# Input and first weights in four pieces, multiplied in step, and a third chunk on the unnormed input

## What is computed

```python
h = rmsnorm(x, mix_pre_norm[l])
u = h @ w_in[l]
u_z, u_xbc, u_dt, u_ly, u_lx, u_g = jnp.split(u, list(IN_SPLITS), axis=-1)
y_a = ssd_mixer(u_z, u_xbc, u_dt, ...)      # causal conv of u_xbc, silu, then a state-space scan
...
g = jax.nn.sigmoid(u_g.reshape(b, s, N_BRANCHES, D_MODEL) + gate_b[l])
```

## Time and profile before

| what | before |
|---|---|
| median of three runs | 841.94 us (841.87 to 842.13) |
| the profiled execution: its time | 842.37 us |
| the profiled execution: its span | 840.5 us |
| PE busy, PEld busy | 828.2 us (99%), 742.4 us (88%) |
| DVE busy, ACT busy, POOL busy | 638.5 us (76%), 503.2 us (60%), 68.3 us (8%) |
| granted TensorE clock, mean | 0.999 |
| HBM over the span | 175 GB/s |

### The profile page before, as it was taken

How to read it: one execution, slowest core, us unless ns; L and a number is a source line. 1 busy time by engine, 2 the same in 40 slices (tenths; PEclk the granted TensorE clock), 3 DMA queues, 4 the chain that set the end, 5 groups by cost and what they waited for, 6 DMA issues and landing times. The chain is left out here.

```text
span 840.5 us, 14554 instructions
## 1 busy us (share of the span) xinstructions
PE 828.2 (99%) x5758; PEld 742.4 (88%) x5758; DVE 638.5 (76%) x1148; ACT 503.2 (60%) x828; POOL 68.3 (8%) x68
## 2 busy tenths in 40 slices
PE   8999999999999999999999999999999999999996
PEld 6999999999989988888888789899899888788885
DVE  6887987998968778878788859777655566776765
ACT  6575778665377755656556868853544363555443
POOL 0200002101020111111111200020000020001000
PEclk9999999999999999999999999999999999999999
DMA  8658443467465746555655455574333433465541
GB/s 299 235 180 285 156 150 109 151 213 285 143 206 161 242 162 210 180 197 176 203 182 197 153 174 199 151 252 151 126 110 118 152 101 101 148 203 181 195 151 51
DMA packets 42812, 147.81 MB, mean 176 GB/s; under 512 B 6876, under 2 KB 7672, under 8 KB 42232
## 3 DMA queue, kind: packets, MB, share of 16 engines
q1 hardware_dynamic: 42600, 146.75, 52.4%
q10 hardware_dynamic: 144, 0.13, 0.0%
HBM read 145.79 MB, written 1.08 MB: 175 GB/s over the span
## 5 line engine op out<-in xcount | busy, mean ns | idle before, releaser
L2000 DVE TENSOR_TENSOR t_wl<-t_raw,t_wh 128x1024 fp32r<-128x1024 f32 x256 | 312.6, 1230 | 84.1 <-ACT t_wh L1423 83.0
L1423 ACT ACTIVATE t_wh<-t_raw 128x1024 fp32r<-128x1024 f32 x256 | 268.1, 1055 | 93.9 <-PE bank L673 91.8
L673 PE MATMUL bank<-t_hx,t_wh 128*128 128x256 f32 (+1 forms) x1968 | 298.5, 302 | 0.3 <-ACT t_hx L1434 0.3
L673 PEld LDWEIGHTS bank<-t_hx,t_wh 128*128 128x128 f32 x1968 | 263.6, 191 | 13.3 <-issue 1.1
L673 PE MATMUL bank<-t_hx,t_wl 128*128 128x256 f32 x1136 | 160.1, 283 | 0.0
L673 PEld LDWEIGHTS bank<-t_hx,t_wl 128*128 128x128 f32 x1136 | 149.2, 192 | 3.0
L673 PE MATMUL bank<-t_wh,t_hx 128*128 128x512 f32 x440 | 122.4, 399 | 0.0
L673 PE MATMUL bank<-t_wh,t_br 128*128 128x512 f32 x384 | 103.9, 392 | 0.0
L673 PEld LDWEIGHTS bank<-t_wh,t_hx 128*128 128x128 f32 x440 | 80.9, 188 | 17.0 <-issue 0.9
L673 PEld LDWEIGHTS bank<-t_wh,t_br 128*128 128x128 f32 x384 | 70.9, 188 | 14.1 <-issue 0.2
L673 PE MATMUL bank<-t_wl,t_hx 128*128 128x512 f32 x220 | 68.3, 392 | 1.0 <-DVE t_wl L2000 1.0
(11 more groups left out here) (149 smaller groups left out, 680.1 us busy)
## 6 DMA issues: line engine op xcount, KB each, us to landing
t_raw<-in_ws SPq DMA_DIRECT2D x258, 512.0 KB, 4.0
t_br<-decay SPq DMA_DIRECT2D x1, 2048.0 KB, 8.8
t_arena<-in_post SPq DMA_DIRECT2D x3, 512.0 KB, 5.2
t_x<-in_xin SPq DMA_DIRECT2D x2, 512.0 KB, 5.1
t_bd<-in_bd SPq DMA_DIRECT2D x1, 1024.0 KB, 7.2
t_x<-in_xtok SPq DMA_DIRECT2D x1, 1024.0 KB, 6.6
t_arena<-in_mem SPq DMA_DIRECT2D x1, 1024.0 KB, 8.7
out<-t_x SPq DMA_DIRECT2D x3, 256.0 KB, 2.3
```

What stands on the lines that cost most here:

```text
L673: return e.matmul(o, l, r, start=st, stop=sp, skip_group_check=True)
L1423: e.activation(high(q), RAW[q % NR][:, :], ACT.Copy, bias=0.0, scale=1.0).then_inc(*hi.now(q))
L2000: e.tensor_tensor(low(q), RAW[q % NR][:, :], high(q).bitcast(F), SUB).then_inc(*lo.now(q))
```

## The change

The input x is loaded in four pieces of two k each (256 KB, rows of 2 KB), and units 0 and 1 in four pieces of 512 columns, alternating with them on SyncE's queue; the columns of `xbc4` are laid out so that piece i holds the weights of k = 2i and 2i+1 for all 256 output columns. ScalarE and VectorE do a piece of x and then its piece of weights, and TensorE multiplies dt and `xbc4` for these two k, four times. The four squares come behind all of this, with no split between them. `xbc0` moves ahead of `g0`, onto the unnormed input: it is now units 4 and 5, `g0` is 6 and 7, `g1` 8 and 9 as before. Its row factor is applied on VectorE as for `xbc4` and `xbc5`; its bank is 4 and its buffer `RAWX[2]`. `mix_sums` moves into `xbc5`, at (0, 3), and `norm_spread` in `xbc5` from (0, 6) to (1, 4). On ScalarE and VectorE, `xbc_first(4)`/`xbc_taps(4)` and `xbc_first(5)`/`xbc_taps(5)` now stand ahead of `g0`'s place in the walk. On VectorE the split of unit 4 moves from inside `h_parts` to ahead of it, and that of unit 5 from behind it to inside.

```diff
@@ stream_list
-    for i in (4, 5):
-        s.append((f"xbc{i}", "w_in", rng(XC_ + 256 * i, 256)))
+    for i in (4, 5, 0):
+        s.append((f"xbc{i}", "by_k" if i == 4 else "w_in", rng(XC_ + 256 * i, 256)))
...
@@ sp_program
-            for i in range(2):
-                e.dma_start(X[:, 4 * i:4 * i + 4, :], xin[:, 4 * i:4 * i + 4, :]).then_inc(s_x[i], 16)
-            fetch(0)
+            for i in range(4):
+                e.dma_start(X[:, 2 * i:2 * i + 2, :], xin[:, 2 * i:2 * i + 2, :]).then_inc(s_x[i], 16)
+                e.dma_start(RAW[i // 2][:, halves(i % 2)], ws[0, :, 512 * i:512 * i + 512]).then_inc(s_early[i], 16)
+            fetch(2)
             e.dma_start(conT[:, 0:NFIRST], con[:, 0:NFIRST]).then_inc(s_con, 16)
-            fetch(1)
+            fetch(3)
...
@@ pe_program
-            for k in range(8):
-                e.wait_ge(*d_xw.of(k))
-                mm(PB[6][0:32, 0:T], DTS[:, k, :], YBh[:, k, :], k == 0, False)
-                m = mm(PB[6][0:16, 0:T], DTS[:, k, 0:16], YBl[:, k, :], False, k == 7)
-            m.then_inc(*p_dt.now("dt"))
-            chunk("xbc4", YBh, YBl, {(0, 4): lambda: e.wait_ge(*hi.of(0)), (1, 6): mix_sums})
-            chunk("xbc5", YBh, YBl, {(0, 6): lambda: norm_spread("mix", 7)})
             for i in range(4):
-                if i == 0:
-                    chunk_by_units("g0", Hh, Hl, normed_high("mix"), normed_low("mix"))
-                    e.wait_ge(*d_const.of("row"))
-                else:
-                    chunk(f"g{i}", Hh, Hl)
+                if i % 2 == 0:
+                    q = walk.unit()
+                wh, wl = weights(q, 4)
+                for k in (2 * i, 2 * i + 1):
+                    e.wait_ge(*d_xw.of(k))
+                    mm(PB[6][0:32, 0:T], DTS[:, k, :], YBh[:, k, :], k == 0, False)
+                    m = mm(PB[6][0:16, 0:T], DTS[:, k, 0:16], YBl[:, k, :], False, k == 7)
...
+                e.wait_ge(*(hi.of(q) if i % 2 else hi.of(q, "first")))
...
+            chunk("xbc5", YBh, YBl, {(0, 3): mix_sums, (1, 4): lambda: norm_spread("mix", 7)})
+            chunk("xbc0", YBh, YBl)
+            chunk_by_units("g0", Hh, Hl, normed_high("mix"), normed_low("mix"))
+            e.wait_ge(*d_const.of("row"))
+            for i in range(1, 4):
+                chunk(f"g{i}", Hh, Hl)
                 chunk(f"xbc{i}", Hh, Hl)
...
@@ act_program
-            for k in range(8):
-                if k % 4 == 0:
-                    e.wait_ge(s_x[k // 4], 16)
-                act(YBh[:, k, :], X[:, k, :], ACT.Copy, scale=WMIX[:, k:k + 1]).then_inc(*a_xw.now(k))
-            split_by_halves(0)
+            for i in range(4):
+                e.wait_ge(s_x[i], 16)
+                for k in (2 * i, 2 * i + 1):
+                    act(YBh[:, k, :], X[:, k, :], ACT.Copy, scale=WMIX[:, k:k + 1]).then_inc(*a_xw.now(k))
+                split_early(i)
             for i in range(4):
                 act(SC0[:, 2 * i:2 * i + 2, :], X[:, 2 * i:2 * i + 2, :], ACT.Square).then_inc(*a_sq.now("mix", i))
-                if i == 1:
-                    split(1)
...
-            for i in range(4):
+            xbc_first(4)
+            walk.cols("xbc0")
+            xbc_first(5)
+            gates(0)
+            for i in range(1, 4):
                 gates(i)
-                xbc_first((4, 0, 1, 2)[i])
+                xbc_first(i - 1)
                 walk.cols(f"xbc{i}")
-                if i == 0:
-                    xbc_first(5)
...
@@ dve_program
-            walk.unit(1)
+            walk.unit(2)
             walk.tick()
-            h_parts("mix", SC1, X, WMIX, 7, {4: 4})
+            h_parts("mix", SC1, X, WMIX, 7, {4: 5})
...
-            for i in range(4):
-                walk.cols(f"g{i}", i == 0)
-                xbc_taps((4, 0, 1, 2)[i])
+            xbc_taps(4)
+            walk.cols("xbc0")
+            xbc_taps(5)
+            walk.cols("g0", True)
+            for i in range(1, 4):
+                walk.cols(f"g{i}")
+                xbc_taps(i - 1)
                 walk.cols(f"xbc{i}")
-                if i == 0:
-                    xbc_taps(5)
```

More of the change, by code:

```diff
@@ L201 @@
 NR, NS = 5, 4
+RAW_CHUNKS = {"xbc4": 0, "xbc5": 1, "xbc0": 2}
 MIDDLE = [name for name, _, _ in STREAM[[s[0] for s in STREAM].index("dnq0"):[s[0] for s in STREAM].index("gt3_0_0")]]
@@ L566, in evacuated @@
                 return (d_ev if name[0] == "vz" else a_ev if name[0][:2] in ("gt", "mv", "vu", "vv") else d_acc).of("free", *name)
-            if name[:2] in ("fu", "lx") or name[:3] in ("xbc", "dnq") and name not in ("xbc4", "xbc5"):
+            if name[:2] in ("fu", "lx") or name[:3] in ("xbc", "dnq") and name not in RAW_CHUNKS:
                 return d_cv.of(name)
@@ L636, in sp_program @@
                     e.wait_ge(s_decay[0], 16)
-                    e.wait_ge(*unit.of(LAST["xbc5"]))
+                    e.wait_ge(*unit.of(LAST["xbc0"]))
                     e.dma_start(ACS, decay.partition_broadcast(P)).then_inc(s_decay[1], 16)
@@ L681, in high_ready @@
             def high_ready(q):
-                e.wait_ge(*(hi.of(q) if q else hi.of(0, "first")))
+                e.wait_ge(*hi.of(q))
             def low_ready(q):
@@ L907, in ssd_lane @@
                     e.wait_ge(*a_silu.of(5))
-                    if g:
-                        e.wait_ge(*d_ssd.of("cb", 0))
+                    e.wait_ge(*(d_ssd.of("cb", 0) if g else d_ev.of("xbc0")))
                     mm(PB[4][:, 0:T], B[:, 0:128], C)
@@ L1231, in pe_program @@
             e.wait_ge(*d_dt.of("w"))
-            for k in range(8):
-                e.wait_ge(*d_xw.of(k))
-                mm(PB[6][0:32, 0:T], DTS[:, k, :], YBh[:, k, :], k == 0, False)
-                m = mm(PB[6][0:16, 0:T], DTS[:, k, 0:16], YBl[:, k, :], False, k == 7)
-            m.then_inc(*p_dt.now("dt"))
-            chunk("xbc4", YBh, YBl, {(0, 4): lambda: e.wait_ge(*hi.of(0)), (1, 6): mix_sums})
-            chunk("xbc5", YBh, YBl, {(0, 6): lambda: norm_spread("mix", 7)})
-            for i in range(4):
-                if i == 0:
-                    chunk_by_units("g0", Hh, Hl, normed_high("mix"), normed_low("mix"))
-                    e.wait_ge(*d_const.of("row"))
-                else:
-                    chunk(f"g{i}", Hh, Hl)
+            for i in range(4):
+                if i % 2 == 0:
[5 more added lines that the diff above has]
+                    m = mm(PB[6][0:16, 0:T], DTS[:, k, 0:16], YBl[:, k, :], False, k == 7)
+                if i == 3:
+                    m.then_inc(*p_dt.now("dt"))
+                cs = [(half(BANK["xbc4"], c), slice(128 * c, 128 * c + 128)) for c in range(2)]
+                e.wait_ge(*(hi.of(q) if i % 2 else hi.of(q, "first")))
+                for k in (2 * i, 2 * i + 1):
+                    for o, w in cs:
+                        mm(o, wh[:, k % 4, w], YBh[:, k, :], k == 0 and w.start == 0, False)
+                        mm(o, wh[:, k % 4, w], YBl[:, k, :], False, False)
+                e.wait_ge(*(lo.of(q) if i % 2 else lo.of(q, "first")))
+                for k in (2 * i, 2 * i + 1):
+                    for o, w in cs:
+                        m = mm(o, wl[:, k % 4, w], YBh[:, k, :], False, k == 7)
+                if i % 2:
+                    m.then_inc(*unit.now(q))
+                    walk.tick()
+            chunk("xbc5", YBh, YBl, {(0, 3): mix_sums, (1, 4): lambda: norm_spread("mix", 7)})
[4 more added lines that the diff above has]
+                chunk(f"g{i}", Hh, Hl)
                 chunk(f"xbc{i}", Hh, Hl)
@@ L1423, in split, with split_early @@
                 e.activation(high(q), RAW[q % NR][:, :], ACT.Copy, bias=0.0, scale=1.0).then_inc(*hi.now(q))
-            def split_by_halves(q):
-                e.wait_ge(s_raw[q], 16)
-                for c in range(2):
-                    e.activation(WH[q][:, halves(c)], RAW[q][:, halves(c)], ACT.Copy, bias=0.0,
-                                 scale=1.0).then_inc(*(hi.now(q) if c else hi.now(q, "first")))
+            def split_early(i):
+                q, c = i // 2, i % 2
+                e.wait_ge(s_early[i], 16)
+                e.activation(WH[q][:, halves(c)], RAW[q][:, halves(c)], ACT.Copy, bias=0.0,
+                             scale=1.0).then_inc(*(hi.now(q) if c else hi.now(q, "first")))
             walk = Walk(split)
@@ L2000, in split, with split_early @@
                 e.tensor_tensor(low(q), RAW[q % NR][:, :], high(q).bitcast(F), SUB).then_inc(*lo.now(q))
[L2002 to L2006 removed]
+            def split_early(i):
+                q, c = i // 2, i % 2
+                e.wait_ge(*(hi.of(q) if c else hi.of(q, "first")))
+                e.tensor_tensor(WL[q][:, halves(c)], RAW[q][:, halves(c)], WH[q][:, halves(c)].bitcast(F),
+                                SUB).then_inc(*(lo.now(q) if c else lo.now(q, "first")))
             walk = Walk(split)
@@ L2976, in lay_out @@
             v = i[c[0]][0][512 * c[1]:512 * c[1] + 512][:, c[2]].reshape(4, P, 512)
+        elif kind == "by_k":
```

(1 more changed line is left out.)

38 lines of the change are left out of this document (17 added, 21 removed).

## The result

| | before | after |
|---|---|---|
| median | 842.04 us (841.87 to 842.38, 4 runs) | 846.54 us (845.74 to 846.70, 4 runs) |
| profiled execution: time, span | 842.37, 840.5 us | 845.74, 843.9 us |
| granted TensorE clock, mean | 0.999 | 0.995 |

The ratio is 1.0051, with a 95% interval of 1.0039 to 1.0063: slower, as forecast, and inside the range. The sum was 3.25 us. Of profiled execution against profiled execution it is 3.37, of the medians 4.5.

What follows compares the result with a forecast made beforehand. TensorE was taken to bound the kernel from 26 us on. A 3.5 us head start less 6.6 to 6.7 us of waits made g1 3.25 us later: 845.2 us against the median, range 843.0 to 847.2.

Steps and rivals of the forecast that it cites:

- The sum: Whole kernel: g1 ends 3.25 us later, added to the profiled 842.37 gives 845.6, or 845.2 against the median.
- The mark at the end of g1: End of unit 9, behind which both orders are the same: 42.40 before, forecast 45.65 with the change.
- T: Start of the normed input on VectorE, forecast at 19.8 against 19.57 before.
- The start: ScalarE and VectorE up to the sums of squares: squares from 11.07, sums read at 15.99, 0.45 earlier than before.
- The landing: Loads of x and weights in pieces: last two at 9.7 and 10.4, nothing added for rows of 2 KB.
- the 1.5 us bound: Loads: the most that rows of 2 KB could delay the last piece, if each 512 KB lose 0.6 us.
- a rival of chance 0.10: Late pieces: rows of 2 KB cost 1.5 us at the last piece, normed input at 21.3, time 846.7; chance 0.10.
- the head start is spent on unit 4's split: VectorE ahead of the normed input: unit 4's split, 1.14 us, moved there, so the norm gains nothing.
- The waits: TensorE in g0 and g1: unit 7 waits 1.7 and 1.75 us, unit 9 waits 2.1 and 0.75.
- The rival of the clock: TensorE's new waits: clock falls to 1.2 GHz for half a unit, 1.4 us more, 846.6; chance 0.06.
- The gain comes through: g0 and g1: splits of units 7 and 9 on time, TensorE keeps its 3.5 us, 838.4; chance 0.10.

Runs made afterwards that it cites:

- the one with TensorE kept busy: The changed kernel with matmuls that nobody reads in TensorE's waits at units 7 and 9: 846.26 us, ratio 1.005 to the kernel before.
- the second profile: The changed kernel timed and profiled once more with no edit: 846.10 us, ratio 1.005 to the kernel before.
- the pieces alone: Loads and engine start of the change, with xbc0, its bank and the splits' order as in the kernel before: 843.66 us, ratio 1.0014.
- the splits ahead: The changed kernel with the splits of units 7 to 11 put back ahead of the convolutions: 840.28 us, ratio 0.9979 to the kernel before.

## Why the prediction was right

The way of the change, the place of the loss and its cause are as forecast: the splits of units 7 and 9 stand in two queues behind the convolutions, and TensorE waits for them. The mark at the end of g1 was T + 25.85, T being the start of the normed input. The change's two profiles and the one with TensorE kept busy give 20.08 and 45.94, 20.75 and 46.60, 20.74 and 46.59: T + 25.86, 25.85 and 25.85. Two terms ahead of T are less good, and they are what the sum of 3.25 lacks: the landing of x, 0.66 us in the second profile, and a wait of VectorE, 0.29. With them g1 would end 4.20 later than before, as it does in that profile.

- **The start.** x came at 4.66 (forecast 4.95), the fourth pair of copies at 9.76 (9.7), the squares at 11.09 (11.07); the sums were read at 15.99, as forecast to the hundredth. That is partly luck: in the second profile the squares start at 11.76 and the sums are read at 16.66. The split of unit 3 started at 17.37 (17.36).
- **T.** Forecast 19.8, measured 20.08 in the profiled run. The splits of units 3 and 4 ended as worked out; then VectorE waited 0.28 more for TensorE's spread of the row factor, which I had put ready at the same moment.
- **The landing was mis-sized.** It is the larger of the two terms that make the median's 4.1 to 4.5 out of 3.25. I took the last piece of x at 9.7 from the 364 GB/s of the earlier trace rows; in the second run its copies start at 10.42, with the pieces alone at 10.14, both after a wait for it. That is up to half of the 1.5 us bound that I set for rows of 2 KB and gave to a rival of chance 0.10. The reason for putting the term at nothing, that the second half of x went faster than the first, compares two loads with rows of the same 4 KB, and so could say nothing on rows of 2 KB. The rival was in part true, and the rate behind it is measured: 246 for 275 GB/s, and 335 GB/s from 7 to 10 us in place of the 364 that the sum used. Why the last piece lands 0.7 us apart in two executions of the same kernel is open.
- **That the head start is spent on unit 4's split** is only half of it. With the pieces alone, where that split is inside the normed input's building, it starts at 19.53: a gain of 0.04, and not of the 0.9 by which 19.8 less the split's 1.14 is ahead of 19.57. The last piece's lateness takes 0.39 of that. The rest is that VectorE, done with unit 3's low part at 18.98, waits 0.55 for TensorE's spread, for which it also waits 0.28 in the changed kernel and 0.54 before. So in each of these profiles it is TensorE that lets the normed input start. With the pieces, TensorE's own way there starts at ScalarE's split of unit 2, behind the four squares. The prediction had this path in its sum, but named the split alone as what the head start is spent on.
- **The waits.** Unit 7: 1.98 and 1.66 us, forecast 1.7 and 1.75. Unit 9's low part: 0.58, forecast 0.75. Unit 9's high part: none, forecast 2.1; ScalarE finished it at 42.25 (forecast 42.0), but TensorE came there only at 42.41, since its clock had fallen. In the second profile the same part is waited for 0.76 us.
- **The rival of the clock** was right in that the clock falls and wrong in its price. It fell for more than the half unit that I assumed (24 matmuls in 4.51 us), yet the run without the fall is no faster. The waits at unit 9 took the loss in.
- **The gain comes through.** This one failed for the queues' order alone, as the reason against it said: with the splits ahead, g1 ends at 38.91 + 0.96 = 39.87, 2.5 us ahead of before, though the time is only 1.8 lower. The difference lies just behind: the next load starts at 40.45 after 0.51 us of idle time that the trace puts down to issue (VectorE's dt lane, on whose buffer `t_sm` this load works, ends at 40.33), and unit 10's at 41.98, 2.00 ahead of its 43.98 before.

## What to carry to other kernels

Work moved ahead of a dependency gains nothing by itself if the splits for what follows stand in an in-order queue behind work that hangs on that dependency. Before moving a chunk, write down for each engine what its queue holds between the dependency and the next thing that the bound engine needs, and move those along: here a few lines of order turned a loss of 4.1 us into a gain of 1.8. A fall of the clock is free only if a later wait absorbs it. So behind a wait look also at the granted clock of the stretch that follows it.
